# Three of four modulations computed as fill steps of three sink-attention tiles instead of in the setup (one core, Trainium2)

## The reference: what is computed

```python
def ada_norm(x, c, w, b, g):
    m = jax.nn.silu(c) @ w + b
    shift, scale, gate = jnp.split(m[:, None, :], 3, axis=-1)
    return rmsnorm(x, g) * (1 + scale) + shift, gate
...
for l in range(DEPTH):
    hp, gp = ada_norm(xp, c_prompt, ada_w[l, 0], ada_b[l, 0], norm_g[l, 0])
    ...                                # mixer: even_mixer (A and B) or odd_mixer (C)
    xp = xp + gp * yp
    hp, gp = ada_norm(xp, c_prompt, ada_w[l, 1], ada_b[l, 1], norm_g[l, 1])
    fp, st_p = conv_ffn(hp, ...)
    xp = xp + gp * fp
```

## Time and profile before

| | us |
|---|---|
| median of 3 runs | 4101.93 |
| lowest, highest | 4093.4, 4102.85 |
| the profiled execution | 4112.55 |
| its span | 4111.0 |
| PE busy in the span | 3575.6 (87%) |
| DVE, ACT, POOL busy | 2129.3, 1365.0, 479.5 |

### The profile page before, as it was taken

How to read it: one execution, slowest core, us unless ns; L and a number is a source line. 1 busy time by engine, 2 the same in 40 slices (tenths; PEclk the granted TensorE clock), 3 DMA queues, 4 the chain that set the end, 5 groups by cost and what they waited for, 6 DMA issues and landing times. The chain is left out here.

```text
span 4111.0 us, 53886 instructions
## 1 busy us (share of the span) xinstructions
PE 3575.6 (87%) x20685; PEld 2102.0 (51%) x20917; DVE 2129.3 (52%) x3527; ACT 1365.0 (33%) x2660; POOL 479.5 (12%) x1002
## 2 busy tenths in 40 slices
PE   6867888777697999999978888888888899999996
PEld 3535455544353555555534555555554455555553
DVE  4644444445445555555545554555544655555553
ACT  5534444344323122222124444444432222122122
POOL 0002122223110000000000222211200000000000
PEclk9888887778798999999989999999998999999998
DMA  7721122112311111111121333333331011111111
GB/s 290 276 59 59 58 83 75 54 47 62 102 35 45 38 47 41 37 47 42 40 66 38 115 115 110 115 105 111 106 114 55 29 47 42 37 47 41 37 37 47
DMA packets 222722, 303.33 MB, mean 74 GB/s; under 512 B 24848, under 2 KB 174969, under 8 KB 221910
## 3 DMA queue, kind: packets, MB, share of 16 engines
q1 hardware_dynamic: 193046, 190.24, 13.9%
q0 software_dynamic: 29504, 110.77, 8.4%
HBM read 264.23 MB, written 63.95 MB: 80 GB/s over the span
## 5 line engine op out<-in xcount | busy, mean ns | idle before, releaser
L96 PE MATMUL psum<-h,ffn_high 128*128 128x512 f32 (+1 forms) x2112 | 1035.9, 531 | 48.2 <-DVE hl L474 48.2
L98 PE MATMUL psum<-hl,ffn_high 128*128 128x512 bf16 (+1 forms) x2028 | 616.6, 337 | 0.0
L100 PE MATMUL psum<-h,ffn_low 128*128 128x512 bf16 (+1 forms) x2066 | 578.9, 332 | 2.9
L96 PE MATMUL psum<-actr,ffn_high 128*128 128x512 f32 (+1 forms) x1056 | 517.2, 530 | 15.7 <-DVE actl L807 15.7
L96 PEld LDWEIGHTS psum<-h,ffn_high 128*128 128x128 f32 x2112 | 409.4, 194 | 135.3 <-issue 43.9
L98 PEld LDWEIGHTS psum<-hl,ffn_high 128*128 128x128 bf16 x2112 | 206.3, 98 | 431.7 <-issue 372.8
L86 PE MATMUL psum<-h,attC_high 128*128 128x384 f32 x744 | 367.5, 494 | 40.2 <-DVE hl L474 23.2
L86 PE MATMUL psum<-h,attAB_high 128*128 128x384 f32 x648 | 333.6, 515 | 39.0 <-DVE hl L474 23.4
L784 DVE TENSOR_SCALAR y<-u,cvT 128x1168 f32<-128x1168 f32 x88 | 78.2, 888 | 530.0 <-ACT u L735 530.0
L98 PE MATMUL psum<-actl,ffn_high 128*128 128x512 bf16 (+1 forms) x1012 | 308.0, 337 | 0.0
L100 PE MATMUL psum<-actr,ffn_low 128*128 128x512 bf16 (+1 forms) x1034 | 290.3, 332 | 1.5
(11 more groups left out here) (441 smaller groups left out, 7129.6 us busy)
## 6 DMA issues: line engine op xcount, KB each, us to landing
ada_raw<-in_ada_w SPq DMA_DIRECT2D x48, 1024.0 KB, 7.7
ffn_raw<-in_w_up SPq DMA_DIRECT2D x88, 512.0 KB, 3.6
ffn_raw<-in_w_down SPq DMA_DIRECT2D x44, 512.0 KB, 3.7
raw_C<-in_cache_c_k POOLq DMA_DIRECT2D x64, 256.0 KB, 3.4
raw_C<-in_cache_c_v POOLq DMA_DIRECT2D x64, 256.0 KB, 3.0
out_ck_s<-in_cache_c_k POOLq DMA_DIRECT2D x8, 1984.0 KB, 8.7
out_cv_s<-in_cache_c_v POOLq DMA_DIRECT2D x8, 1984.0 KB, 14.3
attC_raw<-in_w_in_odd SPq DMA_DIRECT2D x24, 512.0 KB, 4.7
```

The lines of the kernel that those rows point to most:

```text
L96: return pe.matmul(out, w, x[:, lo:hi], start=first and start, stop=last and stop, skip_group_check=True)
L98: return pe.matmul(out, top(w), xl[:, lo:hi], start=first and start, stop=last and stop, skip_group_check=True)
L100: return pe.matmul(out, wl, top(x[:, lo:hi]), start=first and start, stop=last and stop, skip_group_check=True)
```

## The change

Modulation 0 stays in `setup`. The other three are made inside tiles 4, 5 and 6. Each is cut in six units (third j, half h of its 1024 columns), 18 in all, in the order of `ADA`: 7 in tile 4, 4 in tile 5, 7 in tile 6. A unit is four D steps and one M step. A D step uses one 512 KB chunk of the two-slot ring (two rows of k, 512 columns): four matmuls of 512 columns into one PSUM bank; the fourth D step has an ACT copy of 18 x 512 into `modrow`. Each D step is followed by a W step, so its chunk passes ACT and DVE as every chunk does. M is four small matmuls and one DVE addition of the bias into `mod` (for the scale third also `gs`); it comes one unit later than its D steps. `tile_steps` puts units before, between and behind the names of the fill, counts a D step as four and the others as one, and hands out by the floor where it took the ceiling; `late` is now 1 in every tile, so tiles 4 and 6 have places for fill in the first group too. Which of banks 0 and 1 a unit gets, and what it waits for, `place()` works out. The silu rows `cst` and `cb` are kept 18 columns wide, the bias comes by one more small load in the setup and a turn on PE. Some buffers of the AB block shrink or lie elsewhere to make room.

```diff
-FBASE = 4 * 3 * (KT // 2)
+FBASE = 3 * (KT // 2)
+ADA = [(a, j, h) for a in range(1, 4) for j in range(3) for h in range(2)]
+ADA_OF_TILE = {4: ADA[0:7], 5: ADA[7:11], 6: ADA[11:18]}
...
-        for a in range(4):
+        for a in range(1):
             for j in range(3):
                 for c in range(KT // 2):
                     ring.load(sp, ada_chunk(a, j, c), ada_w[a, j, c], view=("p (k n) -> p k n", dict(k=2)))
...
-    late = 0 if fill == "q" else 1
+    late = 1
...
-    todo = [("P", n, b, k) for n in range(KT) for b in range(3) for k in range(KT - 1)] if last else \
-        [("F", name, b, k) for name in fill for b in range(3) for k in range(KT)]
+    todo = [("P", n, b, k) for n in range(KT) for b in range(3) for k in range(KT - 1)] if last else []
+    ada = ADA_OF_TILE.get(T, [])
+    for i in range(len(fill) + 1):
+        for d in range(len(ada) * i // (len(fill) + 1), len(ada) * (i + 1) // (len(fill) + 1)):
+            todo += [("D",) + ada[d] + (q,) for q in range(4)] + ([("M",) + ada[d - 1]] if d else [])
+        todo += [("F", name, b, k) for name in fill[i:i + 1] for b in range(3) for k in range(KT)]
+    todo += [("M",) + ada[-1]] if ada else []
+    upto_ = list(itertools.accumulate(4 if f[0] == "D" else 1 for f in todo))
...
-        upto = -(-len(todo) * seen // total)
+        upto = sent
+        while upto < len(todo) and (seen == total or upto_[upto] * total <= upto_[-1] * seen):
+            upto += 1
...
+                elif what == "D":
+                    a_, j, half, x = s[1:]
+                    ring.load(sp, c, ada_w[a_, 2 * x:2 * x + 2, :, j * D + 512 * half:j * D + 512 * half + 512].rearrange(
+                        "k p n -> p k n"), 0, ("p (k n) -> p k n", dict(k=2)))
+                    spills(c)
...
+                elif what == "D":
+                    x = s[4]
+                    bank, free = at[(T, "D") + s[1:4]]
+                    w, wl = ring.ready(pe, c)
+                    if x == 0:
+                        pe.wait_ge(*free)
+                    out = ps[0:2 * NC9, bank, :]
+                    for i in range(2):
+                        cols = slice(512 * i, 512 * i + 512)
+                        pe.matmul(out, G.cst[:, 2 * x + i, :], w[:, cols], start=(x == i == 0), stop=False)
+                        mm = pe.matmul(out, G.cb[:, 2 * x + i, :], wl[:, cols], start=False, stop=(x == 3 and i == 1))
+                    mm.then_inc(S.t_used[c % 2], 1)
...
+                elif what == "D" and s[4] == 3:
+                    d = ADA.index(s[1:4])
+                    ring.done(act, c)
+                    if d >= 2:
+                        act.wait_ge(S.mod_mm, d)
+                    act.copy(modrow[d % 2], ps[0:2 * NC9, at[(T, "D") + s[1:4]][0], :]).then_inc(S.ada_evac, 1)
```

More of the change, by code:

```diff
@@ L280, in _ @@
         pool.memset(G.mhalf[:, :], -0.5).then_inc(S.set_ones, 1)
[L281 to L284, removed]
+        pool.dma_start(msb[2 * NC9:2 * NC9 + 1, :], ada_b[0:1, :]).then_inc(S.adab_in, 16)
     @block.scalar
@@ L916, in tile_steps @@
             turn, later = later, []
-        steps += todo[sent:upto]
         for f in todo[sent:upto]:
+            if f[0] == "D":
+                steps += turn
+                turn = []
+            steps.append(f)
             if unit_ends(f):
                 turn += [("W",)]
-                later += [("R", f[1])] if f[1] in ("q", "k") else []
+                later += [("R", f[1])] if f[0] == "F" and f[1] != "v" else []
         sent = upto
@@ L1073, in run, with place, take, do @@
                 do_steps(do, kind, T, tile_steps(kind, T, fill, T == TL, nxt), cb + c)
+        def place():
+            turn, last, at = [1], {}, {}
+            def take(key, sem, value):
+                turn[0] ^= 1
+                at[key] = turn[0], last.get(turn[0])
+                last[turn[0]] = sem, value
+            def do(what, kind, T, s, c, turns):
+                if what == "F" and s[3] == 0:
+                    nk, nT = next_tile(kind, T)
+                    name, b = s[1:3]
+                    if T == T0 - 1 and name == "q":
+                        at[T, "F", name, b] = b, None
+                        last[b] = f_sem[name], f_no(name, nk, nT, b)
+                    else:
+                        take((T, "F", name, b), f_sem[name], f_no(name, nk, nT, b))
+                elif what == "P" and s[3] == 0:
+                    take((T, "P") + s[1:3], S.out_evac, 4 * KT * odd + 3 * s[1] + s[2] + 1)
+                elif what == "D" and s[4] == 0:
+                    take((T, "D") + s[1:4], S.ada_evac, 4 + ADA.index(s[1:4]))
+                elif what == "M":
+                    take((T, "M") + s[1:4], S.mod_evac, 2 + ADA.index(s[1:4]))
+                elif what == "VT":
+                    at[T, "VT"] = last[0], last[1]
+                    last[0] = last[1] = S.v_rows, kv(kind, T) + 1
+            run(None, do)
+            return at
         def act_of(T):
@@ L1179, in restore @@
             def restore():
-                ring.done(sp, cb + tiles[-1][3] - 1)
+                ring.done(sp, cb + tiles[6][3] + len(tiles[6][2]) - 1)
                 for t in range(7):
@@ L1385, in do @@
                     pe.wait_ge(S.v_evac, 3 * (n + 1))
+                    for free in at[T, "VT"]:
+                        pe.wait_ge(*free)
                     if not first:
@@ L1614, in _, with split @@
             done = [2 * AB_TENSORS * odd]
-            def split(c, turns):
-                if c + 2 < cb + total or not isinstance(turns, int):
-                    ring.split_high(act, c + 2, turns)
+            turn = [cb + 2]
+            def split():
+                if turn[0] < cb + total:
+                    ring.split_high(act, turn[0])
+                turn[0] += 1
             def do(what, kind, T, s, c, turns):
@@ L1785, in _, with split @@
             dve.wait_ge(S.mask_set, 4 if odd else 2)
-            def split(c, turns):
-                if c + 2 < cb + total or not isinstance(turns, int):
-                    ring.split_low(dve, c + 2, turns)
+            turn = [cb + 2]
+            def split():
+                if turn[0] < cb + total:
+                    ring.split_low(dve, turn[0])
+                turn[0] += 1
             def do(what, kind, T, s, c, turns):
@@ L1794, in do @@
                 if what == "W":
-                    split(c - 1, turns)
+                    split()
                 elif what == "R" and not odd:
```

90 lines of the change are left out of this document (57 added, 33 removed).

## The result

The changed kernel takes 4178.83 us (median of 4 runs, 4173.8 to 4179.82), the kernel before 4099.04 on the same chip (4093.4 to 4102.85): a ratio of 1.0193 [1.0176, 1.0211], slower by 80 us. The forecast was 4086. The profiled execution took 4178.57 (span 4176.5), 66.0 above that of before; before's profiled one lies high, so stages compared in the two traces add up to 66, not to 80.

The account below looks back on a forecast made before the run. PE was taken to bound the setup, a 4.75 us ACT-DVE ring tiles 4 to 6. Saving 121.9 us less 104 + 13 + 6 + 5 - 22 = 106 left 15.9: 4086 (median), range 4045 to 4123.

Parts of the forecast that it names:

- What it takes away: Setup: attention can start after modulation 0 instead of modulation 3, 121.9 us less, with the bias table's DMA chain still hidden.
- In a block: Blocks of tiles 4 to 6: two D steps lengthen 4.75 us to 7.6, 1.45 each, 104 us for 72.
- PE's part of it fits: Blocks with two D steps: PE's 1.9 us for these plus about 2.2 for scores, turn and sums fits in 7.6.
- Units: Tiles 4 to 6: 18 ACT copies and 18 DVE additions cost 13 us; M matmuls lie in PE's room.
- Seams: Tile 5's third chunk loaded behind tile 4's store, 3 us, and two B weights holding the ring, 3: together 6.
- F steps closer together: Stretches between units in tiles 4 to 6: 8 or 9 F steps a block bring PE to 6.4 us; 5 in all.
- rival 3: No gain: packed F blocks in tiles 4 to 6 cost 21 us instead of 5; time 4102, chance 0.24.
- The order of F and P steps: Tiles 0 to 3 and C tiles: F steps move one place at most, lengths stay within 1 us.
- What the new work fills: Tiles 4 and 6: DMA waits filled, 14 us, and a higher PE clock, 8, together 22 us won back.
- Rival 5: Tiles 4 to 6: ACT's waits for chunk landings stop the softmax; cost 157 us, time 4137, chance 0.12.
- Rival 4: Clock: PE stays at 1.2 GHz in tiles 4 to 6; 37 us more, time 4123, chance 0.07.
- The range: Whole kernel: 4045 to 4123 us, leaving out about 2 in 10 of the chances.

Follow-up runs that it names:

- the ceiling and all cuts: Changed kernel, fill handed out by the ceiling, loads 16 of 512 columns, cast/split 64 of 1024, one matmul pair of two, one M matmul of four: 4066.93 us, 0.9897.

## Why the prediction was wrong

- **What it takes away** held: 119.5 against 121.9. The bias table's chain stayed hidden.
- **In a block, 1.45 a D step, 104 in all**: this step failed. The chain of cast and split on ACT and DVE was seen rightly, and a block that ran as I drew it took 8.0 against 7.6. But "PE's part of it fits" was judged by adding up busy time, as if D could slide to where PE is idle. It lies between scores, turn and next scores, waits for its own split, and costs 1.3 us at the upper clock (769.94 to 771.25), 2.1 at the lower, not 0.94, which was read from pairs with 128 columns at the upper clock. Halving it gave back 22 us, which the prediction had at nothing. The work on ACT and DVE, which I took for all of the 104, gave back 59. Loads gave back 20; the load, too, stood in a block's chain (the 1.65 at 753.44).
- **One block for all 72**: I multiplied the cost in a middle block. Only three of tile 4's D steps stand in such a block. At the head of the tile one costs 2.2 us (15 / 7), at the end 3.2 (19 / 6), between the sample groups only 0.4, and in tile 5 3.3 on the mean. There PE was busy 65 of 80 us before; 16 D steps at 1.3 to 2.1 are 21 to 34 us, more than the 15 it had free, so even the sum of busy times spoke against "fits".
- **Units, 13**: the small matmuls gave back 19, so they are not in PE's room either. The row with x4 in the earlier trace rows is two matmuls, not four: each has two records (the 96 of the setup have 192). Four take 1.88 us at the lower clock (762.77), 1.05 at the upper (819.80), and DVE's addition waits for them (the 2.97 at 853.30).
- **Seams, 6**: the wait of which I thought came, 3.16 us of ACT at 877.26 for tile 5's third chunk. But tile 4's end alone took 19 more, where six D steps at 1.45 are 9.
- **F steps closer together, 5**: blocks of F steps alone in tile 4 took 6.6 us, as added up (6.4). In such blocks the price of rival 3 was the right one.
- **The order of F and P steps** ("move by one place at most", within 1 us): failed. The rounding alone is worth 39 us in the changed kernel; with no D step it costs 16 together with the new banks and buffers. The tiles 0 to 3 took 3 us more in all, the C tiles 8.
- **What the new work fills, -22**: not seen. The 14 added up waits of three engines that can run beside each other, and two of the three are there still: ACT waits 3.2 us for `out_bv_s` (at 737.63), DVE 2.7 for its swap (807.74). Tile 4's head became longer by 6.4 us from first to second exponentials, not shorter, and the granted clock of tile 4 stayed at 0.72, while that of tile 6 fell from 0.83 to 0.72.
- **Rivals**: the time lies beyond all of them. Rival 5 had the sign, and a cost (157 us) nearer to 199 than the forecast's 106, and its mechanism in places: in the block shown the landing ends the longer thread. But ACT waits for landings of D chunks only 9.5 us in tiles 4 to 6 together, and short loads give back 20. Rival 4 holds in part. The granted clock of tiles 4 to 6 is 0.72 to 0.74, where tile 5 had 0.88, so many D steps ran at 1.2 GHz: from 748.55 to 750.69 one took 2.14 us. Of the 144 pairs 92 ran at the lower level (0.60 us for the low part's matmul, 0.38 at the upper). The rule cited there from the Trainium skill ("TensorE: Matmul & The Clock Gate", section "HAM oscillation — how this bites in real kernels") is borne out in part: tile 5 fell from 0.88 to 0.74 with 16 D steps in place of none, but not to 0.5. What the clock costs alone was not separated; an estimate of its most is 92 x 0.42 = 39 us for the D steps, if all of them are on the chain.
- **The range** ended at 4123, because its bound of full series, 2.3 us a D step, counted ACT and DVE only. With PE's 1.3 to 2.1 in the same chain it would have been 3.6 to 4.4 us; measured is 199 / 72 = 2.8.

What stays open: with the ceiling and all cuts the steps still cost 119.5 - 42 = about 77 us (42 is 4102 x 0.0103). In it are a matmul pair for each D step (72 at 0.65 to 1.07 us, 47 to 77, if none of it is hidden; the other pair gave 22), the short casts and splits with their hand-overs, R in the middle of the tile, and what the new banks and buffers cost. These were not told apart. So it is shown that PE's part and the M steps do not hide and that ACT and DVE's work is less than a third; the cause of the remaining 77 stays open.

## What to carry to other kernels

Idle time of an in-order engine is free for new work only where the work can stand in its queue without a chained instruction behind it: for each fill step, ask what it waits for and what stands next in that queue, on every engine it touches, and price it in series if both are in the chain. Cost a fill step in each kind of place (head, block, tail) and multiply by how many stand there, not the best block by all: in one tile it was 0.4 to 3.2 us. When a planner's rule is changed along with the work, measure the rule alone with the work left where it was; here it was a fifth of the cost.

## What the runs showed of the hardware that was not expected

- Matmuls with 18 columns of weights cost more than with 128: 0.65 us a pair against 0.47 in the setup, although the high part's weight load itself is shorter. The groups of weight loads in the setup, of the kernel before and of the one with 18 columns there:

```profile
L351 PEld LDWEIGHTS psum<-ada_high,cst 128*128 128x128 f32 x140 | 29.6, 212 | 13.5 <-DVE ada_low L182 10.1 <-issue 3.3
```

```profile
L351 PEld LDWEIGHTS psum<-ada_high,cst 128*18 128x18 f32 x144 | 13.7, 95 | 34.4 <-issue 34.3
```

95 ns instead of 212, but ahead of each load 0.24 us (34.3 / 144) in which nothing in the profile is waited for. What sets that, no run here shows.
- POOL's subtraction of 128x1024 takes 2.39 us, DVE's 1.23.
